# Hybrid NSA and FoX decoder layer on 8 cores: value products issued two tiles later, regrouped gate epilogues, a first load reordered, closing sums spread out

## What is computed

```python
u = rms_norm(h, norm_mix)
q_n, kc, vc, ks, vs, kw, vw, gate_n, q_f, k_f, v_f, f_l = split(u @ w_in)
gates = sigmoid(gate_n)
kcmp, vcmp = compress_blocks(kc), compress_blocks(vc)      # 127 blocks, gelu MLP
o_cmp = masked_softmax(q_n @ kcmp.T) @ vcmp
imp = sum over the 4 heads of a group of p_cmp @ overlap   # 32 blocks of 64 keys
sel_idx = top 16 of imp, with forced blocks
o_sel = softmax over the selected blocks; o_win = softmax over a window of 512
o_n = gates[0] * o_cmp + gates[1] * o_sel + gates[2] * o_win
o_f = masked_softmax(q_f @ k_f.T + forget sums) @ v_f      # 8 heads
y = g_a * (o_n @ w_branch_nsa) + g_b * (o_f @ w_branch_fox)
h = h + y @ w_out
h = h + square(relu(rms_norm(h) @ w_up)) @ w_down
return rms_norm(h)
```

## Time and profile before

| What | us |
|---|---|
| Median of the runs (1222.23, 1223.74, 1354.41) | 1223.74 |
| The profiled execution's own time | 1220.74 |
| Span of its slowest core, first to last instruction | 1219.2 |
| TensorE busy, share of the span | 94% |
| VectorE, ScalarE busy | 52%, 52% |

### The profile page before, as it was taken

How to read it: one execution, slowest core, us unless ns; L and a number is a source line. 1 busy time by engine, 2 the same in 40 slices (tenths; PEclk the granted TensorE clock), 3 DMA queues, 4 the chain that set the end, 5 groups by cost and what they waited for, 6 DMA issues and landing times.

```text
span 1219.2 us, 25543 instructions; the slowest of 8 cores (1214.9 to 1219.2 us)
## 1 busy us (share of the span) xinstructions
PE 1150.7 (94%) x8991; PEld 621.4 (51%) x8991; DVE 637.2 (52%) x1311; ACT 636.9 (52%) x1263; POOL 67.6 (6%) x127
## 2 busy tenths in 40 slices
PE   3988987999999999999999999999999999999995
PEld 2555555575675666754444444444444444444442
DVE  2556777652434434324444366546566564747476
ACT  6546788799998999972222256530211112030354
POOL 0000222111110000000000000000000000000000
PEclk9999999999999999999999999999999999999998
DMA  9952040002020010332131040422211111111034
GB/s 210 244 113 40 7 79 9 2 2 39 2 39 3 5 37 19 97 127 88 21 70 35 1 87 1 86 43 52 45 35 35 35 35 35 35 35 35 1 122 155
DMA packets 18362, 65.91 MB, mean 54 GB/s; under 512 B 4320, under 2 KB 4704, under 8 KB 14016
## 3 DMA queue, kind: packets, MB, share of 16 engines
q0 software_dynamic: 4752, 34.61, 15.6%
q1 hardware_dynamic: 13488, 29.69, 7.8%
HBM read 90.30 MB, written 8.39 MB: 81 GB/s over the span
## 4 chain that ended last, share of the span: by engine, by line
PE 87%; DVE 5%; DMA 4%; issue 3%; ACT 1%; DVEq 0%; SPq 0%; ACTq 0%
PE bank L327 87%; DVE RG L327 4%; DMA RG<-x 4%; ACT RG L327 1%; DVEq L167 0%; ACT L327 0%; DVEq L160 0%; DVE uT L327 0%; SPq L150 0%; ACTq L167 0%; SPq L167 0%
## 5 line engine op out<-in xcount | busy, mean ns | idle before, releaser
L327 ACT ACTIVATE RG<-bank 128x512 bf16<-128x512 f32 (+3 forms) x888 | 463.7, 617 | 354.3 <-PE bank L327 347.3
L327 PE MATMUL bank<-uT,arena 128*128 128x512 bf16 x2048 | 495.2, 379 | 6.6 <-DVE RG L327 4.3
L327 PE MATMUL bank<-RG 128*128 128x65 bf16 (+8 forms) x3860 | 352.6, 228 | 19.3 <-DVE RG L327 13.1
L327 PEld LDWEIGHTS bank<-uT,arena 128*128 128x128 bf16 x2048 | 199.5, 98 | 218.4 <-issue 8.3
L327 DVE TENSOR_TENSOR RG<-RG,bank 128x512 f32<-128x512 f32 x320 | 218.7, 686 | 129.9 <-PE bank L327 125.0
L327 PE MATMUL bank<-arena,RG 128*128 128x512 bf16 x1280 | 279.5, 379 | 0.0
L327 PEld LDWEIGHTS bank<-RG 128*128 128x128 bf16 (+3 forms) x3860 | 198.8, 98 | 119.1 <-issue 51.2
L327 DVE TENSOR_TENSOR RG<-RG 128x512 bf16<-128x512 f32 (+4 forms) x295 | 145.7, 494 | 174.5 <-ACT RG L327 160.6
L327 PEld LDWEIGHTS bank<-arena,RG 128*128 128x128 bf16 x1280 | 124.7, 98 | 148.3
L327 ACT ACTIVATE RG<-RG 128x1 f32<-128x1 f32 (+3 forms) x148 | 85.3, 587 | 69.3 <-DVE RG L327 50.7
L327 ACT ACTIVATE RG<-bank,prm_s 128x512 f32<-128x512 f32 x64 | 43.9, 688 | 116.7 <-PE bank L327 112.1
(11 more groups left out here) (33 smaller groups left out, 260.2 us busy)
## 6 DMA issues: line engine op xcount, KB each, us to landing
arena<-wall POOLq DMA_DIRECT2D x32, 1024.0 KB, 9.3
RG<-x SPq DMA_DIRECT2D x32, 512.0 KB, 12.7
out<-RG SPq DMA_DIRECT2D x32, 256.0 KB, 2.1
RG<-c_qx SPq DMA_DIRECT2D x8, 144.0 KB
RG<-wall POOLq DMA_DIRECT2D x1, 1024.0 KB, 13.1
RG<-RG SPq DMA_DIRECT2D x48, 4.0 KB, 1.7
RG<-c_kx SPq DMA_DIRECT2D x4, 144.0 KB
RG<-c_kx SPq DMA_DIRECT2D x8, 64.0 KB, 1.9
```

What stands on the lines that cost most here:

```text
L327: return P.emit(eng, lambda e, method=method, kw=kw: getattr(e, method)(**kw), ins, outs, inc)
```

## The change

**Value products later.** A constant `LAG` of 2 is added. At step t the loop issues PV and the posts of tile t - 2; S and EXP stay where they were. `PT` has eight buffers in place of six. `COOL` becomes 8.

**Gates.** `gates` keeps 1 + exp(-z); the wide reciprocal goes. An epilogue multiplies the denominator by it, inverts the product and scales. Compressed units of `tg` 2 and 3 invert the bare denominator in one further instruction; that of `tg` 0 clamps and multiplies in one.

**Selection.** The comparison runs once for four query tiles and gives 1 or 0; the -30000 stands in the constant rows `kx` instead.

**Front.** The first x tile is issued before `prm` and the identity; `ss` has 64 bytes per tile; `stageB(0)` and `stageB(1)` follow their own `stageA`; a one-column Ln stands ahead of all ScalarE work.

**Closing sums.** `hst` has 64 bytes per tile, and in the last pass `inv_rms(i - 1)` is issued behind the first half of tile i instead of ahead of it.

```diff
-        NPT = 6
+        NPT = 8
...
+        thr = cv.alloc([8, 8], F32)
...
-        ss = cv.alloc([16], F32)
+        ss = cv.alloc([16, 16], F32)
...
-        P.dma('sp', identb[:, :], cd['c_ident'])
-        P.dma('sp', prm[:, :], prm_d)
         x_tok = []
         for i0 in range(NXS):
             x_tok.append(P.dma('sp', xs[i0], x_d[i0 * 128:(i0 + 1) * 128, :]))
+            if i0 == 0:
+                P.dma('sp', prm[:, :], prm_d)
+                P.dma('sp', identb[:, :], cd['c_ident'])
...
+        E('act', 'activation', out=rstd[:, 0:1], in_=ss[:, 0, 0:1], func=AF.Ln, bias=1.0)
...
         stageA(0)
+        stageB(0)
         stageA(1)
+        stageB(1)
         stageA(2)
-        stageB(0)
-        stageB(1)
...
-        E('dve', 'reciprocal', out=ga, in_=ga)
...
-        COOL = 5
+        COOL = 8
+        LAG = 2
...
-                d['PV']()
-                for f in d['post']:
-                    f()
+                if t >= LAG:
+                    finish(tiles[t - LAG])
+            for t in range(max(n - LAG, 0), n):
+                finish(tiles[t])
...
         def nsa_post(br, h, g, hl, tg):
             def f(ob):
-                r = epi_rec(ob, br == 0 and tg == 0)
                 fs = fsc[ctr['r'] % 2]
-                E('dve', 'tensor_tensor', out=fs, in0=r, in1=gates[:, 4 * tg:4 * tg + 4, br * 8 + h], op=ALU.mult)
+                ctr['r'] += 1
+                ginv = gates[:, 4 * tg:4 * tg + 4, br * 8 + h]
+                den = Obv[ob][:, :, 64]
+                if br == 0 and tg == 0:
+                    E('dve', 'scalar_tensor_tensor', out=fs, in0=den, scalar=1e-30, in1=ginv, op0=ALU.max, op1=ALU.mult)
+                else:
+                    E('dve', 'tensor_tensor', out=fs, in0=den, in1=ginv, op=ALU.mult)
+                E('dve', 'reciprocal', out=fs, in_=fs)
...
                     if tg < 2:
                         return
+                    r = epi_rec(ob)
...
-            E('dve', 'max', out=mx8, in_=sc2)
-            E('dve', 'tensor_scalar', out=selbv[:, g, i, :], in0=score[:, i, :], scalar1=mx8[:, 7:8], scalar2=NEG, op0=ALU.is_lt, op1=ALU.mult)
+            E('dve', 'max', out=thr[:, i, :], in_=sc2)
+            if i % 4 == 3:
+                b = slice(i - 3, i + 1)
+                E('dve', 'tensor_tensor', out=selbv[:, g, b, :], in0=score[:, b, :], in1=thr[:, b, 7:8].to_broadcast([128, 4, 32]), op=ALU.is_lt)
...
-        hst = [cv2.alloc([16], F32) for _ in range(4)]
+        hst = [cv2.alloc([16, 16], F32) for _ in range(4)]
...
         def down(fbs, i):
-            if len(fbs) == 2 and i >= 1:
-                inv_rms(i - 1)
...
                 if len(fbs) == 2:
                     square_sum(i, j)
+                    if j == 0 and i >= 1:
+                        inv_rms(i - 1)
                     if j == 0 and i >= 2:
                         final_tile(i - 2)
```

More of the change, by code:

```diff
@@ L295, in host_consts @@
     kx = np.zeros((2, 36, T), np.float32)
-    kx[0, t // 64, t] = 1.0
+    kx[0, t // 64, t] = NEG
     kx[:, 32:34] = 1.0
@@ L522, in stageA @@
                 x_tok.append(P.dma('sp', xs[b], x_d[i * 128:(i + 1) * 128, :]))
-            E('act', 'activation', out=xn[i % 4], in_=xs[b], func=AF.Square, accum_out=ss[:, i:i + 1])
+            E('act', 'activation', out=xn[i % 4], in_=xs[b], func=AF.Square, accum_out=ss[:, i, 0:1])
         def stageB(i):
@@ L527, in stageB @@
             tb = 3 + i % 3
-            E('act', 'activation', out=rstd[:, i:i + 1], in_=ss[:, i:i + 1], func=AF.Ln, scale=1.0 / D, bias=prm[:, 240:241])
+            E('act', 'activation', out=rstd[:, i:i + 1], in_=ss[:, i, 0:1], func=AF.Ln, scale=1.0 / D, bias=prm[:, 240:241])
             E('act', 'activation', out=rstd[:, i:i + 1], in_=rstd[:, i:i + 1], func=AF.Exp, scale=-0.5)
@@ L765, in run_pipeline, with finish @@
                 tiles[t]['S']()
+            def finish(d):
+                d['PV']()
+                for f in d['post']:
+                    f()
             for t in range(n):
@@ L789, in run_pipeline, with epi_rec @@
                     late = [f for f in late if f.groups]
-                d['PV']()
-                for f in d['post']:
-                    f()
+                if t >= LAG:
+                    finish(tiles[t - LAG])
+            for t in range(max(n - LAG, 0), n):
+                finish(tiles[t])
             while emit_one(n) is not None:
                 pass
-        def epi_rec(ob, clamp):
+        def epi_rec(ob):
             r = rec[ctr['r'] % 2]
-            ctr['r'] += 1
-            if clamp:
-                E('dve', 'tensor_scalar', out=r, in0=Obv[ob][:, :, 64], scalar1=1e-30, scalar2=None, op0=ALU.max)
-                E('dve', 'reciprocal', out=r, in_=r)
-            else:
-                E('dve', 'reciprocal', out=r, in_=Obv[ob][:, :, 64])
+            E('dve', 'reciprocal', out=r, in_=Obv[ob][:, :, 64])
             return r
@@ L830, in f @@
             def f(ob):
-                r = epi_rec(ob, False)
+                ctr['r'] += 1
+                r = epi_rec(ob)
                 E('dve', 'tensor_tensor', out=otm[:, 4 * tg:4 * tg + 4, 512 + h * 64:512 + (h + 1) * 64], in0=Obv[ob][:, :, 0:64], in1=r.unsqueeze(2).to_broadcast([128, 4, 64]), op=ALU.mult)
@@ L1097, in square_sum @@
         def square_sum(i, j):
-            E('act', 'activation', out=sA if j == 0 else sB, in_=h[:, i, HS[j]], func=AF.Square, accum_out=hst[j][:, i:i + 1])
+            E('act', 'activation', out=sA if j == 0 else sB, in_=h[:, i, HS[j]], func=AF.Square, accum_out=hst[j][:, i, 0:1])
         def inv_rms(i):
-            E('dve', 'tensor_tensor', out=hst[2][:, i:i + 1], in0=hst[0][:, i:i + 1], in1=hst[1][:, i:i + 1], op=ALU.add)
-            E('act', 'activation', out=hst[2][:, i:i + 1], in_=hst[2][:, i:i + 1], func=AF.Ln, scale=1.0 / D, bias=prm[:, 240:241])
-            E('act', 'activation', out=hst[3][:, i:i + 1], in_=hst[2][:, i:i + 1], func=AF.Exp, scale=-0.5)
+            E('dve', 'tensor_tensor', out=hst[2][:, i, 0:1], in0=hst[0][:, i, 0:1], in1=hst[1][:, i, 0:1], op=ALU.add)
+            E('act', 'activation', out=hst[2][:, i, 0:1], in_=hst[2][:, i, 0:1], func=AF.Ln, scale=1.0 / D, bias=prm[:, 240:241])
+            E('act', 'activation', out=hst[3][:, i, 0:1], in_=hst[2][:, i, 0:1], func=AF.Exp, scale=-0.5)
         def out_tile(i):
@@ L1117, in v_scale @@
         def v_scale(i):
-            E('dve', 'scalar_tensor_tensor', out=vn[i % 3], in0=h[:, i, :], scalar=hst[3][:, i:i + 1], in1=gmlp, op0=ALU.mult, op1=ALU.mult)
+            E('dve', 'scalar_tensor_tensor', out=vn[i % 3], in0=h[:, i, :], scalar=hst[3][:, i, 0:1], in1=gmlp, op0=ALU.mult, op1=ALU.mult)
         def v_tile(i):
@@ L1153, in final_tile @@
             for j in range(2):
-                E('dve', 'scalar_tensor_tensor', out=ob[:, HS[j]], in0=h[:, i, HS[j]], scalar=hst[3][:, i:i + 1], in1=gfin[:, HS[j]], op0=ALU.mult, op1=ALU.mult)
+                E('dve', 'scalar_tensor_tensor', out=ob[:, HS[j]], in0=h[:, i, HS[j]], scalar=hst[3][:, i, 0:1], in1=gfin[:, HS[j]], op0=ALU.mult, op1=ALU.mult)
                 P.dma('sp', out_d[i * 128:(i + 1) * 128, HS[j]], ob[:, HS[j]])
```

## The result

The changed kernel takes 1203.72 us (median of six runs, 1200.61 to 1206.07). The ratio to the kernel before is 0.984, 95% interval 0.982 to 0.986: 1.6% less time, inside the 2% that counts as no change. The forecast was 1203.0 us, range 1193 to 1214.

A forecast was written before the change was run, and what follows sets the result against it. Loads bound the front, VectorE stage 2's second stretch and nearly its first, TensorE stage 3's filler steps, late VectorE the end. Terms sum to -19.5 us: 1220.74 to 1201.2, plus 2 for the median, 1203; range 1193 to 1214 (8 in 10).

The forecast's parts named there:

- Closing sums: End of the kernel: a cell per tile lets VectorE keep TensorE's pace, so the tail shrinks; -6.2 us (-4.5 to -7.5).
- Second stretch: Stage 2, 166.7 to 220.0 us, bound by VectorE: shorter epilogues -3.3 us and cheaper query selection -1.2, together -4.5 us.
- the selection: Stage 2, tiles 88 to 176: fewer comparisons on VectorE, less two joint ones that come in; net -1.2 us.
- the contention moves to the reciprocal: Stage 2 epilogues: the reciprocal now contends with GpSimd and the 8.7 us of excess stay; 1210.5 us, chance 0.05.
- First stretch: Stage 2, 107.4 to 166.7 us: epilogues take 5.9 us off VectorE, of which -4.5 us was taken.
- my second rival: Only the end counts: filler bursts and a first stretch full on three engines return the epilogues' savings; 1214 us, chance 0.17.
- Change of stage: Around 220 to 230 us: with VectorE less late, most of the filler's bank wait and slow clock goes; -2.5 us.
- Stage 3: Merge in stage 3: steps with fillers are TensorE's, others ScalarE's, slack smooths only narrow tiles; -1.5 us (0 to -5).
- Front: Start of the kernel: first tile squared sooner, but full DMA engines set the chain as before; 0 us (-1.5 to +1).
- The median: Whole time: the runs' median was put 2 us above the sum made against the profiled execution; 1201.2 became 1203.

The follow-up runs named there:

- the version that repairs that error: The changed kernel with COOL 5 up to tile 88 and 8 behind it: ratio to before 0.980, 1089.9 us from tile 0, three runs of 1198.5 to 1201.4 us.

## Why the prediction was right, and where it was not

The sum from tile 0 on was -19.5 us, and the cores' mean lost 19.3. One term was wrong by 5 us and others, each larger than forecast, made up for it: that the total fits to 0.2 us is luck.

**Closing sums, -6.2: right in size.** The tail went from 13.8 to 7.4 us, by the steps worked out: residuals at TensorE's pace, then 0.60, 1.32 and 1.01 us. The expected end, 7.4 us behind TensorE's last matmul, was 7.3. The wait that I named, final tile for the Exp, was only 0.22 us in each tile of before (without it a tile takes 3.63 us for 3.94); the sum's own wait for the square, 0.92 us, which I did not name, is the one that the late position takes away (2.3 us of the tail). Ahead of the last matmul the cells gave 1.3 us where I said 0.3. All of it lies in the output projection and the first steps of the MLP: the matmuls behind the last transposes start 68.5 us after the second table load in before and with both edits undone, 67.2 in after.

**Second stretch, -4.5: it gained 5.3.** At the same clock the gates give 4.2 of it, where I had 3.3; the 1.1 left are near the 1.2 that I gave the selection, but no run shows that it is the selection's. The lag gave nothing here. The price of the new product (153 ns for the 170 taken) and the reciprocal's indifference to GpSimd are as argued. The rival "the contention moves to the reciprocal" is out. The Trainium skill (SBUF — State Buffer, Who interferes with whom) says that a VectorE instruction with two SBUF inputs contends with a GpSimd one that reads SBUF; the traces agree, with 309 and 345 ns for such products against 153 with one operand in PSUM.

**First stretch, -4.5: wrong, it came out at +0.7.** VectorE lost 6.5 us of work there, near the 5.9 forecast. The step that failed is the one on the groups of fillers: "ScalarE has four tiles in hand, 4 x 0.49 = 1.96 us, so it stands at most some 0.2 us eight times". Four is the number of score banks, not of finished scores. ScalarE had one in hand, in one group two, and stood 0.8 to 1.6 us eight times. The trace of before could have told: at two of its groups of 4 nothing was in hand, and ScalarE stood over 1 us. The first of them:

```profile
140.20 5.51 ACT L327 ACTIVATE RG<-bank 128x512 bf16<-128x512 f32 x10 [1.13 <-PE bank L327]
```

COOL 8 costs 3.2 us, and with COOL 5 the stretch takes 54.0. A second term was too large: I let 4.5 us of VectorE's relief reach a stretch that TensorE bounds as well. With lag and COOL undone and the rest kept it takes 54.6 for before's 56.5, so 1.9 us reach it. The lag adds 0.6 beside COOL 5, and -1.9 - 0.6 + 3.2 gives the +0.7. This is what my second rival said of the first stretch; it was wrong on the second.

**Change of stage, -2.5: it gained 4.5, for another reason.** I put it down to VectorE being less late. With lag and COOL undone and the gates kept, the wait stays at 2.64 us and the stretch at 15.1 or 16.7, as the clock falls. It is the lag and the spacing that place the groups where their bank is free.

**Stage 3, -1.5: about -3.3** (1.4 in tiles 198 to 464, 1.9 from there to the table load). The kernel before with the lag alone has 1.3 and 1.8 of it, so there this is the lag's, worth twice what I gave it. Taken out again it gives back less: 2.5 us beside COOL 8, 1.7 beside COOL 5.

**Front, 0: about -2 on the mean core, nothing on the slowest.**

**The median.** I added 2 us between my sum and the median. After, the profiled execution lies 0.7 above the median, not below; my sum against its own time, 1201.2, was 3.3 short. Which core starts stage 2 late is a draw in each execution, and so a single profile's time says less than its part from tile 0 on.

## What to carry to other kernels

When a change takes load off one engine and at the same time makes another's work lumpier, price the lump against what is finished and waiting where it falls, not against the depth of the buffer: an engine that is faster than its supplier has always caught up, here to one tile of four. Give small statistics that two engines pass back and forth a dependency cell each; only then does it help to issue the consumer later, and without that it can cost more than it gives. Read a gain per stretch, cut at the same tile in both kernels, and compare cores whose granted clock was the same: a median over both kinds gave 5.5 us for the gates where 4.2 is theirs at full clock. The split matters: the total here was right to 1 us with a 5 us error in it, and the version that repairs that error takes 3 us off the traces.
